# Expert sum of a sparse layer: every second slot added by VectorE, where it was every fourth

## The reference, cut to what matters

```python
def block(args):
    xt, it, gt = args          # 128 tokens, their 128 expert numbers, their gates
    u = expert_u[it]
    h = jax.nn.gelu(jnp.einsum('td,tkd->tk', xt, u), approximate=False)
    v = expert_v[it]
    return jnp.einsum('tk,tkd->td', gt * h, v)
```

## Time and profile before

| | |
|---|---|
| median of 3 runs | 2047.16 us (2046.88 to 2052.1) |
| profiled execution, its own time | 2054.79 us |
| its span, first to last instruction | 2053.0 us |
| busy share of the span: PE, DVE, ACT, POOL | 84%, 40%, 22%, 15% |
| mean granted TensorE clock | 0.923 |
| adds on DVE (lines 911 and 908) | 64 |
| slots summed by PE (4 matmul records each) | 192 |

### The profile page before, as it was taken

How to read it: one execution, slowest core, us unless ns; L and a number is a source line. 1 busy time by engine, 2 the same in 40 slices (tenths; PEclk the granted TensorE clock), 3 DMA queues, 4 the chain that set the end, 5 groups by cost and what they waited for, 6 DMA issues and landing times.

```text
span 2053.0 us, 17904 instructions
## 1 busy us (share of the span) xinstructions
PE 1730.5 (84%) x6952; PEld 1130.7 (55%) x6952; DVE 816.2 (40%) x1526; ACT 446.8 (22%) x982; POOL 312.0 (15%) x260
## 2 busy tenths in 40 slices
PE   7979988999887778798756867668999889799996
PEld 6837656766465445345422322227886376488852
DVE  2424124421264876635899666661000013310001
ACT  1052114321024343312223322221000012310000
POOL 0000000000002253422345645420000000000000
PEclk9989989996898798899977998989999999999998
DMA  5354211212487799999998999994443343154432
GB/s 197 131 189 186 82 41 42 82 42 92 184 329 279 268 383 398 368 414 424 417 418 321 421 421 422 421 375 168 164 153 138 119 185 123 42 184 164 149 140 100
DMA packets 55184, 471.14 MB, mean 229 GB/s; under 512 B 6592, under 2 KB 7744, under 8 KB 10432
## 3 DMA queue, kind: packets, MB, share of 16 engines
q0 software_dynamic: 36864, 268.45, 31.9%
q1 hardware_dynamic: 18240, 201.60, 26.1%
HBM read 468.98 MB, written 1.05 MB: 229 GB/s over the span
## 4 chain that ended last, share of the span: by engine, by line
PE 60%; DMA 14%; DVE 12%; ACT 4%; issue 4%; POOL 1%; POOLq 0%; DVEq 0%; SPq 0%; ACTq 0%
PE ps L2218 15%; DMA main<-in_expert_uv,main 8%; PE ps L2242 8%; PE ps L469 7%; PE ps L425 6%; DMA panels<-in_expert_uv,main 5%; PE ps L465 4%; PE ps L964 4%; PE ps L1203 4%; DVE main L898 3%; PE ps L2195 3%; PE ps L2199 2%; PE ps L1433 2%; DMA panels<-in_wall 1%; DVE xT L911 1%
## 5 line engine op out<-in xcount | busy, mean ns | idle before, releaser
L880 POOL DMA_INDIRECT main<-in_expert_uv,main x200 | 244.5, 1223 | 970.7 <-DVE main L1733 584.7
L964 PE MATMUL ps<-main 128*128 128x512 f32 x596 | 308.3, 665 | 94.3 <-ACT main L945 94.1
L2218 PE MATMUL ps<-xT,panels 128*128 128x256 f32 x1408 | 304.5, 379 | 0.8 <-DMA panels<-in_wall 0.8
L2218 PEld LDWEIGHTS ps<-xT,panels 128*128 128x128 f32 x1408 | 267.3, 190 | 37.2 <-DMA panels<-in_wall 1.0
L898 DVE SCALAR_TENSOR_TENSOR main<-main 128x1024 f32<-128x1024 f32 x200 | 240.6, 1222 | 111.2 <-DMA main<-in_expert_uv,main 109.9
L964 PEld LDWEIGHTS ps<-main 128*128 128x128 f32 x596 | 121.5, 214 | 262.0 <-ACT main L945 133.5
L2242 PE MATMUL ps<-panels,main 128*128 128x512 f32 x352 | 157.1, 609 | 16.0 <-issue 16.0
L964 PE MATMUL ps<-panels,main 128*128 128x512 f32 x172 | 93.9, 691 | 55.8 <-ACT main L945 49.1
L2293 DVE TENSOR_TENSOR main<-main,ps 128x512 f32<-128x512 f32 x22 | 15.1, 687 | 288.5 <-PE ps L2218 250.5
L2242 PEld LDWEIGHTS ps<-panels,main 128*128 128x128 f32 x352 | 68.7, 196 | 103.2 <-issue 103.1
L425 PE MATMUL ps<-panels,xT 128*128 128x512 f32 x256 | 116.6, 610 | 1.4 <-DVE main L1185 1.4
(11 more groups left out here) (268 smaller groups left out, 1826.7 us busy)
## 6 DMA issues: line engine op xcount, KB each, us to landing
panels<-in_wall SPq DMA_DIRECT2D x88, 2048.0 KB, 7.9
main<-in_rows SPq DMA_DIRECT2D x14, 512.0 KB, 10.2
main<-in_expert_uv,main POOLq DMA_INDIRECT x200, 15.0
main<-in_sub_keys SPq DMA_DIRECT2D x2, 1024.0 KB, 13.2
mats<-in_mats SPq DMA_DIRECT2D x1, 1088.0 KB, 10.1
x<-in_x SPq DMA_DIRECT2D x2, 512.0 KB, 3.8
main<-in_pool_w SPq DMA_DIRECT2D x1, 1024.0 KB, 31.6
main<-in_rel_bias SPq DMA_DIRECT2D x1, 1024.0 KB, 15.1
```

What stands on the lines that cost most here:

```text
L880: pool.indirect_dma_start(out=self.bufs[self.buf_of[r]], out_offset=None, in_=self.c.dram["expert_uv"], in_offset=bass.IndirectOffsetOnAxi ...
L964: mm = pe.matmul(self.c.ps[:, b, :], self.diags[self.of_pe(r) % DIAG_RING], v[:, half * HALF:(half + 1) * HALF], start=(q == 1), stop=(q = ...
L2218: mm = pe.matmul(c.ps[:, bank, t * T:(t + 1) * T], w[:, k, at:at + P], c.xT[:, k, :], start=(k == 0), stop=(k == KC - 1))
```

## The change

One number is changed. The slots with even numbers that are not divisible by four (2, 6, 10 and so on, 64 of 256) go from PE to DVE: their diagonal matrix (945) and their four matmul records on PE go, and an add (911) on DVE comes. Whoever waits for such a slot's buffer now waits for DVE's count of adds instead of PE's count of sums.

```diff
 GROUP = 2
-ADD_EVERY = 4
+ADD_EVERY = 2
 DIAG_RING = 8
 BEHIND = 3
 UV = 2 * D
```

## The result

The changed kernel takes 2061.92 us in the median (2061.73 to 2069.22, 5 runs) where the kernel before, beside it, takes 2046.88. The ratio is 1.0085, interval 1.006 to 1.011: 0.85% slower, where 0.34% was forecast. A second series of 12 executions, against 35 of the kernel before, gives 1.006, interval 1.0037 to 1.0083, with medians 2063.27 and 2049.09. The two differences of medians, 15.0 and 14.2 us, put the loss near 0.7%, about twice the forecast; the two ratios put it at 17 and 12 us.

What follows compares the result with a forecast made beforehand. Gathers (DMA) were taken to pace three stretches, and DVE to bound 986 to 1092 us. The terms -1.7 + 2.4 + 1.0 - 0.7 + 8.0 - 2.1 = +6.9 us took the median 2047.16 to 2054 us; range 2048 to 2063.

Steps and rivals of the forecast that it cites:

- (d): End of hgrn1: without slot 58's PE sum, PE reaches the next matmuls earlier; -0.7 us, between 0 and -2.
- (e): Choice of experts of tile 1: seven new DVE adds delay the gather of slot 142; +8.0 us, bounds 7.1 to 9.0.
- (b): Slots 10 to 25: the DVE adds of 10 and 18 are exposed, others hidden; +2.4 us, bounds 0 and 6.
- (a): Slots 0 to 9: without slot 2's PE sum, the gather behind slot 3's sum comes earlier; -1.7 us, possibly 0.
- (c): Slot 27's gather waits for slot 18's buffer, released later by a DVE add; +1.0 us, between 0 and 3.7.
- (f): Last slots: 254 becomes a DVE add, PE does 4 records instead of 8; -2.1 us, between -1 and -2.7.
- PE, given less to do, runs the end of hgrn1 at half clock: End of hgrn1: PE with less work runs at half clock; about 5 us more; 9% together with DMA running dry.
- PE's relief counts from 838 to 986: 838 to 986 us: PE, not DMA, paces the stretch; slot 104 lands 15.5 us earlier, 2038.6 us in all; 11%.
- DMA runs dry after 1092: After 1092 us: DVE falls behind the landings; some 5 us more, 2059; 9% together with PE at half clock.
- The port of POOL: Gathers into main: every new DVE add holds a gather on POOL; +3 us, to 2057; 5%.

Runs made afterwards that it cites:

- choice_only: Kernel before, but every second slot added by DVE in slots 102 to 126 (7 adds more); ratio 1.0037, 7.6 us.
- early_only: Kernel before, but every second slot added by DVE up to slot 26 (7 adds more); ratio 0.9988, -2.5 us.
- late_only: Kernel before, but every second slot added by DVE from slot 130 on (32 adds more); ratio 0.9983, 3.5 us faster.
- busy_changed: Changed kernel, with PE doing the product for the state's end (line 1461) three times in the mixer of tile 1; ratio to the kernel before 1.0062.
- near_end_only: Kernel before, but slots 46, 50, 54 and 58 also added by DVE (4 adds more); ratio 1.0031, 6.3 us.
- the whole middle: Kernel before, but every second slot added by DVE from slot 28 to slot 100 (18 adds more); ratio 1.002, 4.1 us.

## Why the prediction was wrong

The direction and the main mechanism were right; the size was half of what came. The term that was mis-sized is (d), the end of the mixer.

- **(e), the choice of experts: right.** +8.0 was forecast, with bounds 7.1 to 9.0; `choice_only` costs 7.6 us in time and 8.4 in the trace. DVE stays busy 103.20 us in 106. One part was wrong in detail: the prediction had the gather of slot 142 wait for DVE's first add of tile 1, and it is that of slot 140 that waits, for the add of slot 126. It made little difference in size: from the gather of slot 142 to the dot of slot 180 there are 104.8 and 103.9 us in the changed kernel, 104.0 and 103.9 before.
- **(b): right; (a) and (c): not told apart from the scatter or from (b).** Without the early adds slots 10 to 18 take 31.5 to 31.8 us, with them 33.8 to 34.1: some +2.3, where +2.4 was forecast for the two exposed adds. For (a), the gather of slot 8 starts 53.1 us behind the dot of slot 0 and before 54.9, as -1.8 for -1.7; but over all profiles it is 53.1 to 54.9 with the early adds and 54.6 to 56.8 without. For (c), the gather of slot 27 starts 2.7 us behind the dot of slot 21, where it was 1.3 ahead of it, and the dots of slots 21 and 27 are 15.3 us apart in place of 14.1; the add of slot 22 lies between them, so the +1.2 can be its. What the sum left out is that slot 2 itself is now freed by DVE: the gather of slot 7 comes 8.6 us earlier (46.0 to 37.4 us behind the dot of slot 0). The whole early part, from the dot of slot 0 to that of slot 30, takes 143.6 to 145.5 us with the early adds and 140.6 to 144.0 without, in line with the +1.7 of the three terms; the time of `early_only` (-6.1 to +1.0) shows none of it.
- **(f), the last slots: right.** -2.1 was forecast; `late_only` gains 3.5 us (0.8 to 6.1). In the traces the end takes 5.2 or 6.1 us with the late adds and 6.1 or 7.8 without, so one execution of the changed kernel (6.1) shows no gain over one of the kernel before.
- **(d), the end of the mixer: here it failed.** The step had PE come 1.7 us earlier, -0.7 in sum. In its place the removal of PE sums lengthens PE's idle time ahead of L1474 (to 3.0 us and more, from 0.6), and PE does the mixer's end at half clock: 26.3 to 27.9 us from the first L1474 to the last L1475 in place of 20.3, or of 18.6 where one PE sum between them is gone as well (`busy_changed`). The removal of four of them (`near_end_only`) costs 6.3 us, the whole middle 4.1. With +4.1 in place of -0.7 the forecast's sum would have been 11.7 us, and the second series has 12.3. With the measured times of all parts (7.6, -2.5, +4.1, -3.5) it would be 5.7: their times are too uncertain to close the sum, which the traces do better.
- **Why the rows hid it.** The sum was made against one profiled execution, and in that one the kernel before happened to be at half clock there already: the 0.74 in the earlier trace rows. Against such an execution nothing is lost there (slots 0 to 104 take 390.9 us in it and 387.6 in the changed one), and the whole sum comes out: from slot 0 to L981 the two executions of the changed kernel take 4.7 and 6.7 us more than it, for +6.9 forecast. That is in part luck: slots 0 to 104 are 3.3 and 1.7 us shorter than in it, where +1.0 was forecast, and from the gather of slot 142 to the dot of slot 255 2.2 and 1.7 us are lost, where nothing was. Against the second execution of the kernel before they take 15.5 and 17.5 us more. In the first, PE idled 3.25 us because it had come to L1461 1.65 us earlier behind the dot of slot 50 than in the second, and L1408 1.45 us later, behind dots that waited for their landing. With the work of before in this place 5 of 7 profiled executions are like the second, and the change takes that chance away. The rival that named this ("PE, given less to do, runs the end of hgrn1 at half clock") had the mechanism and a price of 5 us, and got 9% together with another, with the very row as an argument that the clock was low anyway.
- **The rivals.** That PE's relief counts from 838 to 986: no, DMA is at 1.01 there and full in both. That DMA runs dry after 1092: no. The port of POOL: its gathers into main take 1266 ns in the mean against 1223 (1250 against 1230 in the second executions), and the last 88 slots take 218.2 us where they took 218.8; no loss is to be seen from it.

That a loss beyond the forecast lies at the mixer's end is shown by `near_end_only`, in its time; that the half clock is how it comes about is shown by the traces. The one run that gave PE the full clock back in the changed kernel, `busy_changed`, shows it in its trace and not in its time, so how much of the time is the clock's stays open. How often the kernel before goes through at full clock is not measured either: one of its own two profiled executions did, and 5 of the 7 that have the same work there.

## What to carry to other kernels

Before an edit is costed against a profile, ask whether that execution was a typical one: here two profiles of the same kernel differ by 8.4 us in a stretch of 60, and the granted clock of that stretch tells which is which. Work taken off PE where it is not the bound is not free if what follows it is a chain of small matmuls: look at how long PE will wait ahead of them. And a share of DVE's work that is harmless over a whole phase (37 us hidden in the last stretch) costs its full price, 1.2 us an add, in the one stretch where DVE is the bound, so such a ratio is better set by stretch than once for all.

## What the runs showed of the hardware

- PE was at half clock for most or all of the chain of small matmuls after 3.0 to 5.0 us of idling ahead of it (seven executions), and kept full clock after 0 to 1.0 us of idling at the same place (seven executions). The Trainium skill, page "TensorE: Matmul & The Clock Gate", section "HAM oscillation — how this bites in real kernels", tells of matmul bursts that start at the lower clock because PE waited between them. The traces agree that the lower clock follows the longer wait: 0.79 us for two records there, 0.49 after the short one. But only in three of the seven was the first pair slow already (0.71 to 0.77 us); in the others the clock fell some pairs later.
- A PE sum's record took 665 ns in the mean with three PE sums in four slots and 773 with two: a third of the PE sums removed freed 64.7 us of PE and not the 110 to 170 of the prediction.
- Identical instructions before slot 0 took 589 to 601 us over 14 executions, a scatter of 12 us, which is nearly the size of the effect under study. Those from L981 to the end took 660.7 to 667.0 us.
